# A recurrence in chunks with a carried state, and its preparation between projection halves, in a four-layer fp32 model on one core

## What is computed

```python
def step(carry, xs):                       # chunks of 64 tokens
    C, n, m = carry
    d_prev = b + m[..., None]
    d_intra = where(causal, b[:, None] - b[None] + ic[None], -inf)
    m_t = maximum(d_prev, max(d_intra))
    s = einsum('td,sd->ts', qc, kc) * exp(d_intra - m_t)
    num = exp(d_prev - m_t) * (qc @ C) + s @ vc
    qn = exp(d_prev - m_t) * (qc @ n) + sum(s)
    h = num / maximum(abs(qn), exp(-m_t))
    m_new = maximum(b_end + m, max(b_end - b + ic))
    C = exp(b_end + m - m_new) * C + einsum('s,sd,se->de', w_s, kc, vc)
    n = exp(b_end + m - m_new) * n + einsum('s,sd->d', w_s, kc)
```

## Time and profile before

| | |
|---|---|
| three runs | 3835.91, 3841.88, 3842.55 us, median 3841.88 |
| the profiled execution | span 3839.1 us, from first to last instruction; no other time of it is given |
| granted TensorE clock, mean | 0.975 of full speed |
| layer 0: projections, then up to the grid attention | 62.2 to 372.2, then to 550.0 us |
| layer 1: the same | 1371.5 to 1639.1, then to 1794.7 us |

### The profile page before, as it was taken

How to read it: one execution, slowest core, us unless ns; L and a number is a source line. 1 busy time by engine, 2 the same in 40 slices (tenths; PEclk the granted TensorE clock), 3 DMA queues, 4 the chain that set the end, 5 groups by cost and what they waited for, 6 DMA issues and landing times. The chain is left out here.

```text
span 3839.1 us, 38442 instructions
## 1 busy us (share of the span) xinstructions
PE 3607.4 (94%) x14652; PEld 2471.0 (64%) x14652; DVE 2014.0 (52%) x3520; ACT 792.0 (21%) x1624; POOL 1033.6 (27%) x1024
## 2 busy tenths in 40 slices
PE   5999987999999999988799999999999999899999
PEld 4577334555555545833388887478888644578887
DVE  5920567676675550045684446675544333665543
ACT  2101446110010010135511111511111112311110
POOL 0100540322332200033234442034443011044443
PEclk9999999999999999999999999999999999999999
DMA  5522100123332111111022222112222222012222
GB/s 228 166 71 69 37 27 20 57 93 119 116 113 85 55 59 66 55 57 35 17 69 86 88 88 88 66 66 88 88 88 99 77 75 73 2 55 88 88 88 88
DMA packets 54455, 296.99 MB, mean 77 GB/s; under 512 B 6432, under 2 KB 6560, under 8 KB 28160
## 3 DMA queue, kind: packets, MB, share of 16 engines
q1 hardware_dynamic: 38240, 244.32, 18.7%
q10 hardware_dynamic: 9504, 31.46, 2.4%
q0 software_dynamic: 6528, 18.75, 1.5%
HBM read 290.05 MB, written 2.49 MB: 76 GB/s over the span
## 5 line engine op out<-in xcount | busy, mean ns | idle before, releaser
L2205 POOL TENSOR_TENSOR scratch<-ring 128x512 f32<-128x512 f32 (+1 forms) x148 | 187.5, 1267 | 1569.1 <-PE psum L586 1203.6
L586 PE MATMUL psum<-big,scratch 128*128 128x256 f32 (+1 forms) x2240 | 605.6, 426 | 0.0
L561 PE MATMUL psum<-H,ring 128*128 128x512 f32 x1184 | 555.3, 603 | 23.8 <-ACT H L1152 11.5
L586 PEld LDWEIGHTS psum<-big,scratch 128*128 128x128 f32 x2240 | 425.6, 190 | 163.7
L586 PE MATMUL psum<-H,scratch 128*128 128x256 f32 (+1 forms) x1856 | 435.7, 389 | 4.4 <-ACT cb L1082 3.0
L586 PE MATMUL psum<-big,ring 128*128 128x256 f32 (+1 forms) x1520 | 405.6, 419 | 13.7 <-DVE big L1748 4.9
L586 PEld LDWEIGHTS psum<-H,scratch 128*128 128x128 f32 x1856 | 350.6, 190 | 74.5 <-ACT cb L1082 8.5
L586 PE MATMUL psum<-H,ring 128*128 128x256 f32 (+1 forms) x1408 | 375.6, 411 | 9.6 <-ACT H L1152 4.2
L561 PEld LDWEIGHTS psum<-H,ring 128*128 128x128 f32 x1184 | 227.5, 194 | 229.3 <-issue 214.0
L586 PEld LDWEIGHTS psum<-big,ring 128*128 128x128 f32 x1520 | 288.5, 190 | 116.6 <-DVE big L1748 6.5
L586 PEld LDWEIGHTS psum<-H,ring 128*128 128x128 f32 x1408 | 272.6, 194 | 85.0 <-issue 9.5
(11 more groups left out here) (314 smaller groups left out, 4632.3 us busy)
## 6 DMA issues: line engine op xcount, KB each, us to landing
ring<-in_wall SPq DMA_DIRECT2D x202, 1024.0 KB, 5.0
big<-in_wada SPq DMA_DIRECT2D x48, 512.0 KB, 3.6
big<-in_wada POOLq DMA_DIRECT2D x32, 512.0 KB, 4.7
H<-negd ACTq DMA_DIRECT2D x16, 768.0 KB, 5.0
big<-in_wada ACTq DMA_DIRECT2D x4, 2048.0 KB, 20.2
scratch<-in_rpb ACTq DMA_DIRECT2D x16, 448.0 KB, 3.9
X<-in_xin SPq DMA_DIRECT2D x4, 768.0 KB, 11.8
out<-X SPq DMA_DIRECT2D x1, 2048.0 KB, 7.2
```

Source lines behind the costliest of these rows:

```text
L561: mm = pe.matmul(bank(b), lhsT, rhs_x(k0 + k), start=first, stop=last)
L586: mm = pe.matmul(fast_bank(st, q, b), lhsT, rhs(k), start=start and k == 0, stop=k == kt - 1, skip_group_check=True)
L2205: pool.tensor_tensor(s1, a21, a22, ALU.add).then_inc(combo_own, 1)
```

## The change

The recurrence goes by chunks of 128 tokens, six of them, in each direction with a state per head and chunk: scores of a chunk against itself, one product of weighted queries with the state entering it. The states of all chunks are made ahead: the keys are turned to have tokens on partitions (`key_turn`), GpSimd weighs the values for both directions (`weigh_values`), TensorE multiplies (`state_parts`), VectorE carries the state on with a decay (`carry_states`). Gates' turning, rotation, key turns and state products stand in the callback `between` after projection halves. A unit of the new recurrence is a pair of heads and half of the chunks; eight in a layer. The rows that are broadcast are now four kinds in DRAM, and are loaded by SP: decays of a head (`load_w`, five buffers), query weights of a pair (`load_qw`, two buffers). Triangles are added by GpSimd to whole heads. The masks of the first two bias tiles move behind the recurrence's work; their loads wait for six units.

```diff
@@ SP, after the fetch of slot s of a layer
+            def recurrence_loads(l, s):
+                if s == 8:
+                    sp.wait_ge(gate_e, l + 1)
+                    for i in range(2):
+                        sp.dma_start(negd[2 * i:2 * i + 2].rearrange("d r t -> (d r) t"), rows[i]).then_inc(rows_out, 16)
+                elif s == 13:
+                    sp.wait_ge(rows_out, 32 * (l + 1))
+                    load_w(l, 1)
+                elif s == 14:
+                    sp.wait_ge(delta_done, 4 * l + 4)
+                    load_w(l, 0)
+                    load_qw(l, 0)
+                elif s == 16:
+                    load_w(l, 2)
+                    load_w(l, 3)
+                    load_qw(l, 1)
+                    load_w(l, 4)
+                    sp.wait_ge(pv_done, 8 * l + 2)
+                    load_w(l, 5)
+                    load_qw(l, 2)
+                    sp.wait_ge(pv_done, 8 * l + 4)
+                    load_w(l, 6)
+                    load_w(l, 7)
+                    load_qw(l, 3)
@@ TensorE
             def gates_turn(l):
-                pe.wait_ge(gate_m, l + 1)
+                pe.wait_ge(gate_e, l + 1)
+                for b, src in ((4, rows[4]), (5, rows[5]), (7, rows[2])):
+                    for t in range(TT):
+                        pe.transpose(psum[:, b * 512 + t * 64:b * 512 + (t + 1) * 64], src[:, t * P:(t + 1) * P],
+                                     ident[0:64, 0:64])
...
+                        for i in range(2):
+                            mm = pe.matmul(psum[64 * i:64 * i + 64, at:at + TT], ident[0:64, r + i:r + i + 1].to_broadcast([64, 64]),
+                                           small[0:64, 108:114], start=True, stop=True, skip_group_check=True)
+                mm.then_inc(gates_T, 1)
+            def key_turn(l, j):
...
+                for x in range(2):
+                    t = 2 * j + x
+                    for f in range(4):
+                        at = (4 + x) * 512 + f * P
+                        mm = pe.transpose(psum[:, at:at + P], KM[:, f, t * P:(t + 1) * P], ident)
+            def state_parts(l, p):
...
+                    for i in range(2):
+                        h = 2 * p + i
+                        mm = pe.matmul(psum[64 * i:64 * i + 64, at:at + 130], KT[:, t, h * HD:(h + 1) * HD], VW[:, t, i, :],
+                                       start=True, stop=True, skip_group_check=True)
+                scores(0)
+                from_states(0)
+                for u in range(8):
+                    if u < 7:
+                        scores(u + 1)
+                    within(u)
+                    if u < 7:
+                        from_states(u + 1)
@@ TensorE, scores(u), from_states(u), within(u)
+                            mm = pe.matmul(psum[:, at:at + P], KM[hp, p, t * P:(t + 1) * P], QM[hp, p, t * P:(t + 1) * P],
+                                           start=True, stop=True)
...
+                    pe.wait_ge(qs_ready, 4 * l + p + 1)
+                    if u >= 2:
+                        pe.wait_ge(num_read, 8 * l + u - 1)
...
+                                    pe.matmul(out_cols(u, i, 2 * n + d), QW[p % 2][hp, d, t * P:(t + 1) * P], CS[hp, p, t, d, :],
...
+                        pe.wait_ge(p_ready, 16 * l + 2 * u + i + 1)
...
+                                mm = pe.matmul(out_cols(u, i, 2 * n + d), WB[W_OF[h]][:, d, t * P:(t + 1) * P], VM[:, t, h, :],
@@ TensorE, after the halves of project (j = 2 * s + f) and of project_tokens
+                        if j == 10:
+                            gates_turn(l)
+                        elif j > 11:
+                            rope(l, j - 12)
...
+                        if j < 2:
+                            rope(l, 2 * j + 4)
+                            rope(l, 2 * j + 5)
+                        elif j < 5:
+                            key_turn(l, j - 2)
+                        elif 6 <= j < 10:
+                            state_parts(l, j - 6)
@@ ScalarE
+            def key_copy(l, j):
...
+                for u in range(8):
+                    p, tl = u // 2, chunk_group(l, u % 2)
+                    for i in range(2):
+                        h = 2 * p + i
+                        act.wait_ge(w_tri, 8 * l + h + 1)
+                        for t in tl:
+                            for d in range(2):
+                                x, c = WB[W_OF[h]][:, d, t * P:(t + 1) * P], t * 64 + 32 * d + h
+                                ins = act.activation(x, x, ACT.Exp, bias=aT[:, c:c + 1])
+                        ins.then_inc(w_exp, 1)
+                act.wait_ge(pv_done, 8 * l + 6)
+                for h in range(2):
+                    load_bias(l, h)
@@ VectorE
+            def weigh_queries(l, p):
...
+                dve.wait_ge(qw_in[p % 2], 32 * (2 * l + p // 2 + 1))
+                dve.tensor_tensor(x, x, QM[:, p, t0:].unsqueeze(1).to_broadcast([P, 2, TOK - t0]), ALU.mult)\
+                   .then_inc(qs_ready, 1)
...
+                for u in range(8):
+                    weights(u)
+                    if u % 2 == 0 and u < 6:
+                        weigh_queries(l, u // 2 + 1)
+                    if u:
+                        finish(u - 1)
+                finish(7)
@@ VectorE, program of a layer
                 rope(l)
+                dve.wait_ge(gates_Ts, l + 1)
+                for p in range(4):
+                    carry_states(l, p)
+                weigh_queries(l, 0)
                 mlstm(l)
@@ GpSimd
+                for p in range(4):
+                    weigh_values(p)
+                for h in range(NH):
+                    b, n = w_loaded(l, h)
+                    pool.wait_ge(w_in[b], n)
+                    t0 = CHUNKS[l][0] * P
+                    for d in range(2):
+                        x = WB[b][:, d, t0:].rearrange("p (t c) -> p t c", c=P)
+                        ins = pool.tensor_tensor(x, x, tri[d].unsqueeze(1).to_broadcast([P, len(CHUNKS[l]), P]), ALU.add)
+                    ins.then_inc(w_tri, 1)
                 for h in range(2):
                     add_mask(h)
```

More of the change, by code:

```diff
@@ L646, in fast_stage, with project_tokens @@
                 w.fast += len(slots)
-            def project_tokens(lhs, with_ctx):
+            def project_tokens(lhs, with_ctx, after=None):
                 r = wait_slot()
@@ L663, in project_tokens @@
                     w.unit += 1
+                    if after is not None:
+                        after(f)
                 w.slot += 1
@@ new lines, in within @@
+                def within(u):
+                    p, tl = u // 2, chunk_group(l, u % 2)
+                    for i in range(2):
+                        h = 2 * p + i
+                        pe.wait_ge(p_ready, 16 * l + 2 * u + i + 1)
+                        for n, t in enumerate(tl):
+                            for d in range(2):
+                                mm = pe.matmul(out_cols(u, i, 2 * n + d), WB[W_OF[h]][:, d, t * P:(t + 1) * P], VM[:, t, h, :],
+                                               start=False, stop=True, skip_group_check=True)
+                    mm.then_inc(pv_done, 1)
@@ L1046, in half, with copy_units @@
                 act.wait_ge(half_done, w.halves(f))
-            def copy_units(dsts, scale, with_ctx, slots=1):
+            def copy_units(dsts, scale, with_ctx, after=None):
                 buf, f0 = dsts
-                w.slot += slots - 1
                 for f in range(2):
@@ L1195, in out @@
                     act.activation(H[:, 4 + p, t0:t0 + n], psum[:, 3584:3584 + n], ACT.Copy).then_inc(nY, 1)
-                act.wait_ge(pv_done, sum(NH * JOBS[i] for i in range(l + 1)))
+                act.wait_ge(pv_done, 8 * l + 8)
                 for h in (2, 3):
@@ L1839, in rope, with carry_states @@
                     dve.tensor_tensor(x, x, t, ALU.add).then_inc(rope_done, 1)
-            def mlstm(l):
-                jobs = mlstm_jobs(l)
-                nj, j0 = len(jobs), l * NH * JOBS[0]
-                t0 = 0 if l == 0 else CT
-                nt = TT - t0
-                def finish(h):
-                    dve.wait_ge(num_turned, l * NH + h + 1)
-                    sums = psum[:, 3072:4096].rearrange("p (d w) -> p d w", d=2)[:, :, t0 * 65:TT * 65]\
-                        .rearrange("p d (t c) -> p d t c", c=65)
-                    den = small[:, 16:28].rearrange("p (d t) -> p d t", d=2)[:, :, t0:]
-                    rden = small[:, 32:44].rearrange("p (d t) -> p d t", d=2)[:, :, t0:]
-                    guard = eT[:].rearrange("p (t d r) -> p d t r", d=2, r=32)[:, :, t0:, h]
-                    step(dve.tensor_copy(den, sums[:, :, :, 64]))
+            def carry_states(l, p):
+                dve.wait_ge(delta_done, 4 * l + p + 1)
+                onward = ((0, 1, 2, 3, 4, 5), (1, 0, 5, 4, 3, 2))
+                for d in range(2):
+                    own(dve.tensor_copy(CS[:, p, onward[d][1], d, :], delta_of(p, onward[d][0], d)))
+                own.wait()
```

(7 more changed lines are left out.)

475 lines of the change are left out of this document (235 added, 240 removed).

## The result

| | before | after |
|---|---|---|
| runs of the comparison | 3835.44 to 3842.55 us, median 3838.89 (4) | 3685.52 to 3690.54 us, median 3689.96 (4) |
| profiled execution | span 3839.1 us | 3690.07 us, span 3688.2 us |
| mean granted clock of TensorE | 0.975 | 0.959 |

The ratio is 0.9609, with a 95% interval from 0.9596 to 0.9623: 149 us faster. Forecast were 3712 us within 3675 to 3755. In the profiles 150.9 us are gained between the spans.

The account below looks back on a forecast made before the run. TensorE was taken as the bound. Recurrences of 86 and 64 us plus twice 27 us of moved work make 204 against 333.4 us: gain 129.4, span 3709.7, forecast 3712 us, range 3675 to 3755.

Parts of the forecast that it names:

- What bounds the kernel: Whole kernel: TensorE, busy 94% of the span, is the bound; an edit is worth what it shortens there.
- Moved between halves: Gate turns, rotations, key turns and state products between projection halves cost TensorE 27 us a layer, bounds 20 and 35.
- State products: Between projection halves: 48 products of 130 columns at 1.18 ns a column, 7.4 us, taken as 10 with gaps.
- 2.4 us a layer: Recurrence: changes of tile on TensorE, two a unit at 0.15 us each.
- The recurrence: New recurrence, last projection product to grid attention: 86 us in layer 0, 64 in layer 1, against 333.4 us old.
- The three hand-overs: Recurrence: VectorE waits for each pair's query weights ahead of work TensorE needs; layer 0 pauses 0 to 12, 4, 6 us.
- The row of transfers: SP's loads ahead of query weights: 2.1 us for each in the row in layer 0, 1.4 in layer 1.
- The clock step: Recurrence: each pause puts some 5 us of TensorE's next work at half speed; 8 us in layer 0, 6 in layer 1.
- Slower than before: Rival, chance 0.03: TensorE stays at 1.2 GHz through both recurrences; at 0.72 us a product, 3858 us.
- Weight loads don't overlap: Rival, chance 0.15: each small recurrence product costs 0.38 us; 3741 us, or 3750 with hand-overs uncovered too.
- GpSimd under VectorE's traffic: Rival, chance 0.15: triangles cost 7.2 us a head, value weights 8 us a pair; +15 us, 3727.
- Smoother: Rival, chance 0.12: early transfers, clock at 2.4 GHz, row halves overlapping fully; 3686 us.

Follow-up runs that it names:

- e5: The kernel after, with the state products of both heads of a pair written to the same 64 partitions (even heads' states lost): 3697.54 us.
- e12: The kernel after, with ScalarE's copy of the gate rows put back ahead of the copies of projection slot 0: 3701.16 us.
- e1: The kernel after, with VectorE weighing the next pair's queries one unit later, behind the finish of the unit before: 3653.30 us.
- e9: e7 plus two 512-column products that nobody reads behind each unit but the last: 3637.47 us.
- e7: e1 plus query weights issued ahead of decays in each group, and the first group of transfers ahead of the last 1 MB slot: 3652.44 us.
- e4: The kernel after, with rotations, key turns and state products run behind the last projection half instead of between halves: 3768.68 us.

## Why the prediction was right, and where its terms were off

**What bounds the kernel: right.** The gain is TensorE's own, 149.0 us of busy time, and moved TensorE work was not hidden but moved.

**Moved between halves: right in kind, far too dear.** Forecast 27 us a layer with bounds 20 and 35. TensorE's busy time in the projections grew by 15.4 us (304.66 to 320.10) in layer 0 and 16.5 (262.54 to 279.04) in layer 1, below the lower bound. Term by term in layer 0: the gates' turns and products were taken at 1.8 + 3.4 and took 1.3 + 1.0 = 2.3 (186.85 to 189.15): 0.23 us was the price of a product bound by loading a 128x128 weight, and these with 64 rows and columns take 0.06. Rotations: 8, measured 6.8 (four pairs at 1.71). Key turns: 3.6, measured 2.6 (three groups of 0.87). State products: 10, measured 5.9 (four groups of 1.48), because these alternate between the two halves of the partitions. All in one half they take 11.2 (e5: four of 2.81), at 0.23 us a product; the price of 1.18 ns a column, 7.4 us in all, was the wrong measure for either. Together 17.6 by starts. Busy time grew by less, since in the kernel before it held some 3 us of products at half clock behind the pause.

**A part of the change was not costed.** "The projections have hardly any idle time" was read from the earlier trace rows, and the 5.3 and 5.1 us that they did have were not followed to their cause: a half's copy on ScalarE, queued behind the gate rows, which the diff moves. That is worth 10.4 us by the pauses alone, 11.2 by the medians of e12 and 16.0 by its stretches, which include the products at half clock behind them. With it the projections grew by 10.1 and, from their first product, 11.4 us only.

**The Trainium skill** (TensorEngine Tiling (Array Packing), Key Properties) says that tiles work independently, so that one can load and multiply beside another. For halves of the columns e5 agrees: 1.48 against 2.81 us. Its other sentence, that a change of tiling mode drains TensorE, stood behind 2.4 us a layer. No run here isolates that: the rows of e1 show TensorE busy in 62.30 of 62.30 us across more than a dozen changes, in which a drain could be hidden, and the term is neither confirmed nor refuted.

**The recurrence: 86 and 64 forecast, 91.4 and 69.4 measured, 5.4 too little in each.** The three hand-overs stood where the prediction put them, with VectorE's finish queued behind the wait. Their times were short: query weights landed 15.0 us after the last projection product (12.0), and 9.8 and 13.3 us after their issue began (7.4 and 9.5). The row of transfers was costed by two loads issued together; the line of after says 6.1 us at the least, 8.8 in the median and 12.7 at the most.

**The clock step failed.** It said that each pause "puts some 5 us of the next work at half speed" and charged 8 and 6 us. For wide products that is what the trace of before shows, half clock from 100.25 to about 105.5 us behind the pause of 5.33. Here the 1.2 GHz held nearly throughout instead, 0.54 in each recurrence, and e1 shows 62.3 us at 0.50 with no pause in them: the clock fell and did not come back. TensorE's busy time in layer 0 is 69.2 us, where 61 + 8 + 2.4 = 71.4 was forecast: nearly the right sum by luck, from parts that were off both ways, since the prediction had far too little at half clock and took each product at 0.28 us and each score at 0.25. The idle time is 22.2 us (three pauses of 17.4, the rest at both ends), where it had 14.5 (75.5 less 61). At full clock the twelve within a chunk take 2.73 us in e9, 0.23 each, at half clock 5.31 (422.17 to 427.48), 0.44 each; the six scores take 0.82 and 1.55.

**The rivals.** *Slower than before*: its condition, half clock all through, came true, though not by a wait behind each small group, as e1 shows. Its price did not: 0.44 us a product against its point of 0.68, as it argued against itself, "below 0.61". That is why the kernel is faster all the same. *Weight loads don't overlap*: falls, 0.23 us at full clock and not 0.38. *GpSimd under VectorE's traffic*: falls. The value weights and the triangles, GpSimd's lines after (ns: least, median, most):

```profile
L2382 POOL TENSOR_TENSOR scratch<-big,num_b x16: 1488/1500/1502, 272.0 to 1539.8; 128x780 f32<-128x780 f32 x16
...
L2397 POOL TENSOR_TENSOR H<-H,con x20: 1085/1314/1544, 389.3 to 1616.3; 128x768 f32<-128x768 f32 x10, 128x512 f32<-128x512 f32 x10
```

The 1.8 us of the prediction were enough, and the doubling of the earlier trace rows appeared once, as 3.058 us among eight triangles in `wx`. The contention that the Trainium skill (GPSIMD Engine Reference, 1. Specifications) states for VectorE's instructions with two SBUF inputs hardly shows in GpSimd's times. It shows in VectorE's: 1.02 us in place of 0.17 in e7 and, in the kernel after, one step of the finish (L2000) that takes 1.29 us once, beside a triangle, and 0.17 otherwise in layer 0. *Smoother*: no, though e1 and e9 are that case and more.

In sum, against the forecast's 3709.7 us of span: moved work 22.1 us less (54 against 31.9 of busy time), ScalarE's order 10.4 less, recurrences 10.8 more, which is 21.7 us less, and the span is 21.5 us shorter. That the total came this near is partly luck: a third of the first two errors was made up by the recurrences, and ScalarE's order was not in the sum at all.

## What to carry to other kernels

An in-order engine that waits for a transfer should do first whatever another engine waits for: here two lines swapped are worth 36.7 us, a quarter of what the whole restructuring gained. Steps in which several engines hand over to each other belong between long stretches of the bounding engine, even if its own part costs the same there (e4: 78.7 us). And in a stretch of small products read the granted clock before anything else: halving their number may halve nothing if they run at 1.2 GHz, and a stretch whose bounding engine is 100% busy can still have a good deal to give (a unit of 9.5 us became 6.8, added work and all, and layer 0's recurrence went from 73.7 to 59.5 between e7 and e9).

## What the runs showed that was not expected

Adding products that compute nothing made the kernel faster. Two 128x512 products behind each of seven units, 1.87 us each time, brought the granted clock of layer 0's recurrence from 0.50 to 0.93 and the unit from 9.5 to 6.8 us. One a unit brought nothing, three cost more than two, and two of 384 columns came out at either level. The Trainium skill (TensorE: Matmul & The Clock Gate, Part 1: The HAM clock gate) puts the lower level down to an engine that was idle and the higher to one that was kept busy. In the kernel before, the rows agree: after 2.41 us without work the clock was 0.56. In e1 they agree in part at most: the clock fell behind the short pauses at the start, but then it stayed at 0.50 through 62.30 us of which all 62.30 were busy by the profile. What the runs show is which streams brought it back: products of 65 and 128 columns alone did not, the same with two or more wide ones among them did, and so did the projections' wide products behind the pause in the kernel before. Whether it is the share of streamed columns, the weight loads or something else that tells them apart was not separated.
